# SSD of a hybrid encoder trunk: earlier in the layer, in 64-column tiles, gate in four steps, cumulated decays spread by DMA

## What is computed

```
h = rms_norm(x, norm1); proj = h @ w_in
aq, ak, av, iq, ik, iw, bq, bk, bv, cz, cxbc, cdt = split(proj)
x = x + concat[A(sparse attention), B(band attention), C(SSD)] @ w_out
u = relu(rms_norm(x, norm2) @ w_up);  x = x + (u * u) @ w_down
```

```
xs, bs, cs = silu(causal_dwconv(xbc))
dt = softplus(dt_raw + dt_bias);  a_cs = cumsum(dt * a)         # per head, along the tokens of a tile
y = (cb * exp(segsum)) @ (xs * dt) + (cs * exp(a_cs)) @ state    # cb[l,s] = cs[l].bs[s]
g = (y + d_skip * xs) * silu(z)
out = group_rms_norm(g) * gate_norm                              # 4 groups of 256 columns
```

## Time and profile before

| what | value |
|---|---|
| median of 3 runs | 3183.55 us |
| the profiled execution, its time | 3184.23 us |
| its span in the trace | 3182.1 us |
| mean granted TensorE clock | 0.985 of full |
| TensorE busy | 3111.2 us (98%) |
| VectorE busy | 1721.0 us (54%) |
| ScalarE busy | 1115.8 us (35%) |
| GpSimd busy | 99.9 us (3%) |

### The profile page before, as it was taken

How to read it: one execution, slowest core, us unless ns; L and a number is a source line. 1 busy time by engine, 2 the same in 40 slices (tenths; PEclk the granted TensorE clock), 3 DMA queues, 4 the chain that set the end, 5 groups by cost and what they waited for, 6 DMA issues and landing times.

```text
span 3182.1 us, 52698 instructions
## 1 busy us (share of the span) xinstructions
PE 3111.2 (98%) x20829; PEld 3055.1 (96%) x20829; DVE 1721.0 (54%) x2264; ACT 1115.8 (35%) x1296; POOL 99.9 (3%) x108
## 2 busy tenths in 40 slices
PE   8999999899999999999999999998999999999998
PEld 8899998799999999999999999987999999999998
DVE  5674567774444444444566645587644443444454
ACT  3343543233333233333323435432332332333333
POOL 1000000010000000000110000000100000000001
PEclk9999999899999999999999999998999999999999
DMA  7444443144444444444443443422444444444442
GB/s 211 143 153 132 134 146 107 60 146 139 151 149 149 152 146 151 148 148 151 147 136 118 160 141 123 157 87 81 139 147 152 147 150 150 147 151 147 150 149 95
DMA packets 234964, 444.41 MB, mean 140 GB/s; under 512 B 23216, under 2 KB 23664, under 8 KB 234848
## 3 DMA queue, kind: packets, MB, share of 16 engines
q1 hardware_dynamic: 229424, 426.37, 41.9%
q0 software_dynamic: 5424, 16.43, 1.7%
HBM read 430.94 MB, written 12.85 MB: 139 GB/s over the span
## 4 chain that ended last, share of the span: by engine, by line
PE 67%; issue 28%; DVE 3%; DVEq 1%; ACT 1%; POOLq 0%; DMA 0%; SPq 0%; ACTq 0%
PE G L675 20%; PE G L677 20%; PE G L676 20%; PE M L712 1%; PE M L955 1%; PE M L849 1%; PE M L903 1%; DVE raw_parts L1341 1%; PE M L957 0%; POOLq L535 0%; PE M L794 0%; PE M L775 0%; DVE X L1756 0%; PE M L703 0%; DMA U<-in_x_sample 0%
## 5 line engine op out<-in xcount | busy, mean ns | idle before, releaser
L1341 DVE TENSOR_TENSOR raw_parts<-raw,whi 128x1024 fp32r<-128x1024 f32 (+1 forms) x816 | 977.2, 1207 | 1085.5 <-ACT whi L1072 1071.7
L1072 ACT ACTIVATE whi<-raw 128x1024 fp32r<-128x1024 f32 (+1 forms) x816 | 851.5, 1045 | 1437.9 <-PE G L677 1401.7
L675 PE MATMUL G<-X_parts,whi 128*128 128x320 f32 x3840 | 1200.5, 313 | 7.8 <-DVE TB L1855 3.8
L677 PE MATMUL G<-X_parts,raw_parts 128*128 128x320 f32 x3840 | 1189.2, 310 | 0.0
L676 PE MATMUL G<-X_parts,whi 128*128 128x320 f32 x3840 | 1188.9, 310 | 0.0
L675 PE MATMUL G<-U_parts,whi 128*128 128x320 f32 x2560 | 798.6, 312 | 11.2 <-DVE U_parts L1532 11.1
L676 PE MATMUL G<-U_parts,whi 128*128 128x320 f32 x2560 | 793.7, 310 | 0.0
L677 PE MATMUL G<-U_parts,raw_parts 128*128 128x320 f32 x2560 | 793.3, 310 | 0.0
L675 PEld LDWEIGHTS G<-X_parts,whi 128*128 128x128 f32 x3840 | 723.4, 188 | 14.9 <-DVE raw_parts L1341 4.5
L676 PEld LDWEIGHTS G<-X_parts,whi 128*128 128x128 f32 x3840 | 723.6, 188 | 0.4
L677 PEld LDWEIGHTS G<-X_parts,raw_parts 128*128 128x128 f32 x3840 | 723.3, 188 | 0.0
(11 more groups left out here) (265 smaller groups left out, 1315.4 us busy)
## 6 DMA issues: line engine op xcount, KB each, us to landing
raw<-in_w_up SPq DMA_DIRECT2D x256, 512.0 KB, 3.6
raw<-in_w_down SPq DMA_DIRECT2D x256, 512.0 KB, 3.6
raw<-in_w_in SPq DMA_DIRECT2D x224, 512.0 KB, 3.4
raw<-in_w_out SPq DMA_DIRECT2D x64, 512.0 KB, 3.6
U<-in_x_prompt SPq DMA_DIRECT2D x8, 256.0 KB, 7.3
out_y_prompt<-U SPq DMA_DIRECT2D x8, 256.0 KB, 2.2
bias_ext<-XC POOLq DMA_DIRECT2D x2, 768.0 KB, 5.4
raw<-in_w_in SPq DMA_DIRECT2D x16, 80.0 KB, 2.0
```

What stands on the lines that cost most here:

```text
L675: pe.matmul(out, hi, xh, start=(i == 0 and k == 0), stop=False)
L677: mm = pe.matmul(out, lo, xh, start=False, stop=(c == part[1] - 1 and k == KC - 1))
L1072: act.activation(whi[:, c % 4, :, cols], raw[:, c, :, cols], ACT.Copy).then_inc(high_done.sem, 1)
L1341: dve.tensor_tensor(wlo[:, c, :, cols], raw[:, c, :, cols], whi[:, c % 4, :, cols].bitcast(F32), ALU.subtract)\
```

## The change

Five things change, in the words of the code.

- **Order.** The z units follow xbc in `PROJ`; SSD starts at slot 107, three slots after the last xbc unit, in steps of one and a half slots; due slots of y run from 109 to 125, of the gate from 124 to 129.
- **bc.** The matmuls are gone. GpSimd writes the 16 rows of cumulated decays to DRAM once a layer and reads them back for each step with a broadcast over 128 partitions into two buffers BC.
- **y.** A matmul for each head, 64 columns wide, two heads of a pair on the two halves of the PSUM partitions; `MM` and `CTS` are gone, weights are made in place; XC takes y in place of `YT`, z is multiplied once a group at t = 2.
- **Gate.** Four steps of one group each, on all three engines.
- **Small.** The unit "small" uses 96 columns in place of 128, and the rope of the second indexer-query unit (`finish` of unit 1) moves from the slots of "small" to those of the unit after it.

Buffers move to other parts of the same memory (XD, BT, BC, EX, EB to U; H0, SO to MIX; ST to TB), and the load of the old state (H0) is issued when the operands of A and B are made.

```
 PROJ = [...
-        ("z", COL_Z, 0), ("z", COL_Z + UNIT, 1),
         ("xbc", COL_XBC, 0), ("xbc", COL_XBC + UNIT, 1), ("xbc", COL_XBC + 2 * UNIT, 2),
-        ("xbc", COL_XBC + 3 * UNIT, 3)]
+        ("xbc", COL_XBC + 3 * UNIT, 3), ("z", COL_Z, 0), ("z", COL_Z + UNIT, 1)]
...
-    at = SLOTS_PROJ + 3
+    at = CHUNKS * (Q_CONV + 1) + 3
     due["last"] = due["cb"] = at
     for t in range(3):
-        due["tile", t] = at + 5 * t
         for g in range(C_GROUPS):
-            due["y", t, g] = at + 5 * t + g + (t < 1)
-        due["so", t] = at + 5 * t + 5
-    due["gate"] = at + 17
+            due["y", t, g] = at + 2 + (3 * (C_GROUPS * t + g)) // 2
+        due["tile", t] = due["y", t, 0] - 1
+    for t in range(3):
+        due["so", t] = due["y", t, C_GROUPS - 1] + 1
+    for g in range(C_GROUPS):
+        due["gate", g] = due["y", 2, g] + 3
+        due["rms", g] = due["gate", g] + 1
...
+            pool.wait_ge(acst_ready.sem, acst_ready.at(l, 1))
+            pool.dma_start(acs_rows[l], ACST).then_inc(acs_out.sem, 16)
+            pool.wait_ge(acs_out.sem, acs_out.at(l, 1))
+            def spread(k):
+                if k >= 2:
+                    pool.wait_ge(ex_ready.sem, ex_ready.at(l, k - 1))
+                pool.dma_start(BC[:, k % 2, 0:HPG * n].rearrange("p (j s) -> p j s", j=HPG),
+                               acs_rows[l:l + 1, HPG * g:HPG * g + HPG, o:o + n].broadcast_to([P, HPG, n]))
+            spread(0)
+            spread(1)
...
+            for k in range(2, len(groups)):
+                spread(k)
...
-                    for j in range(HPG):
-                        mm = pe.matmul(mb(key)[:, j * n:(j + 1) * n], ident[0:C_HEADS, h:h + 1].broadcast_to([C_HEADS, P]),
-                                       ACST[:, o:o + n], start=True, stop=True)
...
-                        out = mb(key)[:, 2 * p * n:2 * (p + 1) * n]
-                        mm = pe.matmul(out, XD[0:n, f:f + P], MM[0:n, k % 2, 2 * p * n:2 * (p + 1) * n], start=True, stop=(t == 0))
-                        if t:
-                            mm = pe.matmul(out, ST[:, f:f + P], CTS[:, k % 2, 2 * p * n:2 * (p + 1) * n], start=False, stop=True)
+                        for from_state in range(2 if t else 1):
+                            for half in range(2):
+                                j = 2 * p + half
+                                f = (HPG * g + j) * C_HD
+                                out = mb(key)[C_HD * half:C_HD * (half + 1), p * n:(p + 1) * n]
+                                cols = slice(j * n, (j + 1) * n)
+                                if from_state:
+                                    mm = pe.matmul(out, ST[:, f:f + C_HD], EB[k % 2][:, cols], start=False, stop=True)
+                                else:
+                                    mm = pe.matmul(out, XD[0:n, f:f + C_HD], EX[0:n, k % 2, cols], start=True, stop=(t == 0))
...
+                    if t:
+                        filled(act, l, ("y",) + groups[k - 2])
+                        act.wait_ge(bc_in[k % 2].sem, bc_in[k % 2].at(l, k // 2 + 1))
+                        act.activation(EB[k % 2][:, 0:HPG * n], BC[:, k % 2, 0:HPG * n], ACT.Exp)
                     act.wait_ge(diff.sem, diff.at(l, k + 1))
-                    act.activation(e_, e_, ACT.Exp).then_inc(ex_ready.sem, 1)
+                    for j in range(HPG):
+                        ins = act.activation(e_, e_, ACT.Exp, bias=NACS[0:n, t, h:h + 1], scale=1.0)
+                    ins.then_inc(ex_ready.sem, 1)
...
+                for g in range(C_GROUPS):
+                    yield due["gate", g] - 1
+                    gate_square(g)
+                    yield due["gate", g]
+                    gate_root(g)
...
-                    for j in range(HPG):
-                        ins = dve.scalar_tensor_tensor(out=e_[:, j * n:(j + 1) * n],
-                                                       in0=mb(("bc", t, g))[0:n, j * n:(j + 1) * n],
+                    dve.wait_ge(bc_in[k % 2].sem, bc_in[k % 2].at(l, k // 2 + 1))
+                    dve.tensor_tensor(EX..., BC..., tri[0:n, 0, 0:n]..., ALU.add).then_inc(diff.sem, 1)
...
+                for g in range(C_GROUPS):
+                    yield due["rms", g]
+                    gate(g)
...
-                if 0 < q <= Q_OUT and 2 <= c < 5:
-                    finish(q - 1, c - 2)
+                if 0 < q <= Q_OUT and q != Q_SMALL and 2 <= c < 5:
+                    finish(q - 1 if q != Q_SMALL + 1 else Q_SMALL - 1, c - 2)
```

More of the change, by code:

```diff
@@ L84 @@
 Q_SMALL = [k for k, _, _ in PROJ].index("small")
+Q_CONV = [(k, h) for k, _, h in PROJ].index(("xbc", 3))
 R_IW = IDX_DIM
@@ L396, in trunk @@
     acst_ready = Count(nc, "acst_ready", 1)
+    acs_out = Count(nc, "acs_rows_out", 1, step=16)
+    bc_in = [Count(nc, f"acs_broadcast_in{i}", 6, step=16) for i in range(2)]
     dend_in = Count(nc, "dend_in", 1)
@@ L409, in trunk @@
     so_out = Count(nc, "state_rows_stored", 2, step=16)
-    gz = Count(nc, "gated", 1)
+    gz = Count(nc, "gated", 4)
     gsq = Count(nc, "gate_squares", 4)
@@ L918, in tile, with gate @@
                     transposes(l, key, [(mb(key)[0:n, b * P:(b + 1) * P], XC[:, 8 + b, at:at + n]) for b in range(4)])
[L920 to L928, removed]
+                def gate(g):
+                    pe.wait_ge(gsq.sem, gsq.at(l, g + 1))
+                    key = ("gs", g)
+                    free_bank(pe, l, key)
+                    for b in range(2):
+                        mm = pe.matmul(mb(key)[:, 0:TOK], ones[:], SQZ[:, 2 * g + b, :], start=(b == 0), stop=(b == 1))
+                    done_filling(mm, key)
                 yield due["last"]
@@ L974, in mixers @@
                         tile(t + 1)
-                yield due["gate"]
-                gate()
+                for g in range(C_GROUPS):
+                    yield due["gate", g]
+                    gate(g)
             mix = Steps(mixers())
@@ L1206, in tile, with gate_square, gate_root @@
                     act.drain().then_inc(bt_ready.sem, 1)
-                def gate():
-                    act.wait_ge(gz.sem, gz.at(l, 1))
-                    for g in range(C_GROUPS):
-                        act.activation(SQZ[:, 2 * g:2 * g + 2, :], Z[:, 2 * g:2 * g + 2, :], ACT.Square).then_inc(gsq.sem, 1)
-                    for g in range(C_GROUPS):
-                        key = ("gs", g)
-                        filled(act, l, key)
-                        drained(act.activation(GRMS[:, g, :], mb(key)[:, 0:TOK], ACT.Sqrt, scale=1.0 / (C_WIDTH // C_GROUPS),
-                                               bias=eps[:, 0:1]), key)
-                        act.drain().then_inc(grms.sem, 1)
+                def gate_square(g):
+                    if g == 0:
+                        act.wait_ge(x_free.sem, x_free.at(l, 1))
+                    act.wait_ge(gz.sem, gz.at(l, g + 1))
+                    act.activation(SQZ[:, 2 * g:2 * g + 2, :], Z[:, 2 * g:2 * g + 2, :], ACT.Square).then_inc(gsq.sem, 1)
+                def gate_root(g):
+                    key = ("gs", g)
+                    filled(act, l, key)
+                    drained(act.activation(GRMS[:, g, :], mb(key)[:, 0:TOK], ACT.Sqrt, scale=1.0 / (C_WIDTH // C_GROUPS),
+                                           bias=eps[:, 0:1]), key)
+                    act.drain().then_inc(grms.sem, 1)
                 decays(0, 0)
@@ L1803, in mixers @@
                         tile(t + 1)
-                dve.drain().then_inc(gz.sem, 1)
-                yield due["gate"]
-                gate()
+                for g in range(C_GROUPS):
+                    yield due["rms", g]
+                    gate(g)
             mix = Steps(mixers())
```

122 lines of the change are left out of this document (61 added, 61 removed).

## The result

The changed kernel takes 3107.13 us (median of 4 runs, 3104.95 to 3108.34); the kernel before took 3183.66 beside it. The ratio is 0.9762 (95% interval 0.9745 to 0.9779): 76.5 us less, where 80 were forecast, 3 us above the predicted 3104 and inside the range. The profiled execution took 3107.04 us.

What follows compares the result with a forecast made beforehand. TensorE, busy 98% of the span, was taken as the bound. The terms -25.9 - 15.6 - 27.7 - 13.0 + 2 = -80.2 from 3184.2 us gave 3104 us, with a range of 3080 to 3130.

Steps and rivals of the forecast that it cites:

- bc, -25.9: SSD steps: bc's matmuls leave TensorE's queue, 1.08 us in each of 12 steps in 2 layers, 25.9 us less.
- y, -15.6: SSD steps: y's 64-column tiles run side by side, saving 0.35 us at t = 0, 0.8 at t > 0; 15.6 less.
- Idle time and slow clock, -27.7: SSD and gate: early SSD and a four-step gate leave 30 of 57.7 us idle or slow clock, 27.7 less.
- the waits forecast at slots 126 and 128: TensorE at the gate: 1.7 us for state copy and squares, 1.4 for the root, 6.0 for the residual.
- The small ones: TensorE's shorter waits in SSD: 2.3 us at slot 124, 0.5 at slot 112, 0.2 for the tile of t = 2.
- What is added elsewhere, +2: Other engines: broadcasts and added ScalarE work hidden, convolution taps meet the band attention; 2 us more, bounds 0 and 10.
- "small", -13.0: Unit "small": its rope, moved into later slots, is hidden; 6.5 us less, twice, 13.0 in all, bounds 9.1 and 15.2.
- The signs that the forecast named: No waits of 3 us or more behind slot 135, SSD some 46 us a layer, "small" some 8 at clock 1.00.
- turns: Rival on y: column tiles take turns, y gains nothing and the form's change costs 2.4 us; 3122 us, chance 0.15.
- VectorE as the bound: Rival on SSD: VectorE's work makes TensorE wait in every step, 24 steps of 1 us; 3128 us, chance 0.10.
- the gate at the end: Rival: y or the gate still falls behind slot 135, all 27.7 us are lost; 3132 us, chance 0.01.
- The hidden gate, 3082: Rival on the gate: VectorE's and ScalarE's lead covers its waits, 30 us become some 8; 3082 us, chance 0.10.

Runs made afterwards that it cites:

- run 2: The changed kernel with the four bc products of every step issued again on TensorE, broadcasts by DMA kept: 3136.39 us.
- run 3: The changed kernel with y's products reordered, all of one column half first, then all of the other: 3116.39 us.
- run 6: The changed kernel with the due slots of SSD and gate as in the kernel before; broadcasts, 64-column tiles and unit order stay: 3129.95 us.
- run 7: The changed kernel with every broadcast from the third on issued one step later: 3112.09 us.
- run 5: The changed kernel with the reading out of "small"'s sums moved ahead of the split of the second chunk behind "small": 3099.97 us.
- run 4: The changed kernel with the four gate steps at slots 127, 129, 131 and 133 instead of 124 to 127: 3089.3 us.

## Why the prediction was right, and where it was not

- *bc, -25.9.* Right: 1.08 us a step by run 2 (1.03 at t = 2), on the path.
- *y, -15.6.* Right in kind, a little large. At t = 1 it is 1.83 less 1.02, the 0.8 of the forecast. At t = 2 I had taken the same; there y took 1.67 us before (593.13 to 594.80) and takes 1.05 now (516.43 to 517.48), by the timelines of TensorE:

```profile
593.13 0.49 PE L955 MATMUL M<-X 64*128 64x128 f32 x2
...
594.80 0.70 PE L961 MATMUL M<-X 64*128 64x256 f32 x2
```

```profile
516.43 0.33 PE L980 MATMUL M<-U 64*64 64x64 f32 x4
516.69 0.34 PE L978 MATMUL M<-U,TB 128*64 128x64 f32 x4
...
517.48 0.70 PE L984 MATMUL M<-U 64*128 64x256 f32 x2
```

  So 0.6 in place of 0.8: with half the columns a group of four still takes 0.26 us, where it takes 0.22 to 0.31 at t = 1. The products here alternate between 64 and 128 rows, and in run 3 a group of two takes 0.26 as well; that the alternation sets this time is likely, but no run takes it away. With t = 0 as forecast the term is (4 x 0.35 + 4 x 0.8 + 4 x 0.6) x 2 = 14.0. The Trainium skill's page "TensorEngine Tiling (Array Packing)", section "Key Properties", says that tiles run independently and that a change of the mode drains TensorE. Run 3 bears out the first at t = 0 and t = 1, and the gap of 0.31 us from cb to y, for 0.22 of two instructions at pace, fits the second, as does t = 2 in run 3, where nothing overlaps.
- *Idle time and slow clock, -27.7.* Right, and not by luck of a sum: the waits forecast at slots 126 and 128 were 1.7, 1.4 and 6.0, and are 1.70, 1.47 and 5.26. Following VectorE's queue from the first root gave 12.3 us for 11.9. The small ones were less sure: 2.3 at slot 124 is 1.18, 0.5 at slot 112 is 0.18, 0.2 for the tile of t = 2 is 0.87. Together 10.7 us a layer, for 12.1. What the stretches gave beyond bc and y is 69.4 - 25.9 - 14.0 = 29.5; this is a remainder, and run 6, which takes the early SSD away by itself, gave 22.8 over its runs.
- *What is added elsewhere, +2.* Nothing of it shows in TensorE's waits; the broadcasts are hidden, by less than I had thought (run 7: one step less is felt, where the forecast had 14 us of cover for a landing of 5.7).
- *"small", -13.0.* Wrong: 6.2, below the bound of 9.1. The failed step is "Moved into slots of 3.5 us each, where a split takes 1.22, it is hidden ... I leave 1.1 for the reading out". It asked what covers the rope, and left 1.1 us a layer for what is late next, the reading out of "small" itself. That stands behind a split whose weights are still on their way: TensorE waits 3.9 and 2.4 us for it, and the clock is low behind (0.88 and 0.93 in the stretches). Run 5 took it away and got 8.1 us in the same stretches: 14.3 with the 6.2, so the forecast's size was there to be had, but not by this change alone.
- The sum. 80.2 were forecast and the spans differ by 76.8; it is this near because misses offset each other in part. "small" was 6.8 too large and y 1.6, while the idle time gave 1.8 more, the 2 added elsewhere didn't show, and 1.2 came from other places.
- The signs that the forecast named: behind slot 135, from 590 to 640 us in the first layer, TensorE has no wait and the clock is 1.00; SSD costs 47.3 us a layer for "some 46", and the new wait is where it was put. "small" at a clock of 1.00 didn't come.
- The rivals: turns fell (run 3), VectorE as the bound fell (it stood idle for 6.28 us just ahead of the long wait, and run 4 fits the same work in), the gate at the end is run 6. The hidden gate, 3082, was not what this change does, but it is what run 4 does with other due slots: 3089.3.

## What to carry to other kernels

When work is moved off the end of a queue, follow the engine that feeds the waiting one instruction by instruction: here the sum of what stands ahead of the residual on VectorE gave the new wait within 1 us. Run 4, which takes that wait away by two lines of the schedule, gained 13.2 us in its stretches, about as much as all the 64-column tiles (14.0). A short reading out that frees a bank belongs ahead of work that may wait for a transfer. And count a wait of TensorE with the slow matmuls behind it: in run 4 the waits for residual and squares are 9.4 us shorter and the stretches 13.2, in run 5 4.5 and 8.1.

## What was not expected of the hardware

Column halves of TensorE can run ahead of their place: in run 3, at t = 1, a product of the second half started beside the third of the first, past a fourth issued ahead of it. At t = 2, with row counts that alternate, none did (2.05 us for 1.05).

The granted clock can fall with no wait of TensorE near. The changed kernel in its first layer, and at the same point of the work in its second (from the last of the band attention's products on 64 columns):

```profile
382.00:388.00 6.00, 6.00 (x31) 5.93 (x31) 4.93 (x5) 4.24 (x5) 0.00 (x0) 0.72 0.13 51
```

```profile
1913.51:1919.51 6.00, 6.00 (x41) 5.93 (x41) 4.93 (x5) 5.32 (x6) 0.00 (x0) 1.00 0.24 64
```

TensorE is busy throughout, yet issues 31 matmuls for 41, which is 1.5 us lost. In run 5 it is the other way round: 1.00 in the first layer, 0.72 in the second. Run 2 shows the fall in the first layer too, run 4 in neither, with the same work. So falls of this size at a few such places come and go within one execution, and may be why the times of a kernel spread by several us; what decides them stays open.
